# Seven half-size products in place of eight for the feed-forward gate units of a two-model forward pass

## The reference, cut to what matters

```python
D_MODEL = 1024; SEQ = 512; DEPTH = 2
D_FF = ((8 * D_MODEL // 3 + 255) // 256) * 256        # 2816

def swiglu(h, w_gate, w_up, w_down):
    return (jax.nn.silu(h @ w_gate) * (h @ w_up)) @ w_down

def first_block(x, ...):
    for i in range(DEPTH):
        h = rms_norm(x, mix_norm[i])
        x = x + (short_conv_mixer(...) if i % 2 == 0 else dilated_attention_mixer(...))
        h = rms_norm(x, ffn_norm[i])
        x = x + swiglu(h, ffn_w_gate[i], ffn_w_up[i], ffn_w_down[i])
    return rms_norm(x, final_norm)
```

## Time and profile before

| | |
|---|---|
| median of three runs | 2059.03 us (2058.18 to 2061.39) |
| the profiled execution | 2057.88 us |
| its span in the trace | 2055.9 us, so 2.0 us lie around the span |
| TensorE matmuls busy | 2024.0 us, 98% of the span |
| GpSimd busy | 1032.9 us, 50% |
| VectorE, ScalarE busy | 896.8 us, 840.8 us |
| gate and up of layer 0 / its down product | about 204 to 433 us / 433 to 553 us |
| the same of layer 1 | about 810 to 1040 us / 1040 to 1159 us |

### The profile page before, as it was taken

One profiled execution on the slowest core, in us unless ns is written; L12 is line 12 of the kernel. 1 busy time (PEld: TensorE's weight loads), 2 busy tenths in 40 slices (PEclk: granted clock), 3 DMA queues, 4 the chain that ended last, 5 costly groups with the idle time before them and its releaser, 6 DMA issues.

```text
span 2055.9 us, 25781 instructions
## 1 busy us (share of the span) xinstructions
PE 2024.0 (98%) x9884; PEld 1654.1 (80%) x9884; DVE 896.8 (44%) x1411; ACT 840.8 (41%) x1341; POOL 1032.9 (50%) x855
## 2 busy tenths in 40 slices
PE   9999999999999999999999999999999999999998
PEld 7888888888877777888888778988887876677787
DVE  3184433322144435334322388778875215443331
ACT  4123222222244443222222377677774325544543
POOL 4455544545532224544545468788885441323242
PEclk9999999999999999999999999999999999999999
DMA  5223233223433312333233334434432321112131
GB/s 169 97 87 113 83 103 103 84 84 97 126 91 93 92 42 82 103 103 102 84 89 101 102 105 123 122 104 114 133 103 62 105 84 62 60 63 81 43 103 62
DMA packets 259365, 193.28 MB, mean 94 GB/s; under 512 B 9459, under 2 KB 247335, under 8 KB 259256
## 3 DMA queue, kind: packets, MB, share of 16 engines
q1 hardware_dynamic: 256188, 190.67, 30.9%
q10 hardware_dynamic: 3068, 1.09, 0.2%
HBM read 189.46 MB, written 2.27 MB: 93 GB/s over the span
## 4 chain that ended last, share of the span: by engine, by line
PE 38%; issue 35%; POOL 21%; DVE 2%; ACT 2%; DMA 1%; POOLq 0%; SPq 0%; ACTq 0%; DVEq 0%
POOL wlo L652 21%; PE bank L2058 11%; PE bank L2060 11%; PE bank L2059 11%; PE bank L2541 1%; PE bank L2537 1%; PE bank L2505 1%; DMA raw<-in_conv_w_in 0%; DVE xc L1668 0%; ACT whi L741 0%; DVE hLo L1971 0%; DMA rows<-cums 0%; PE bank L2519 0%; PE bank L2493 0%; PE bank L2477 0%
## 5 line engine op out<-in xcount | busy, mean ns | idle before, releaser
L652 POOL TENSOR_TENSOR wlo<-raw,whi 128x512 fp32r<-128x512 f32 (+1 forms) x664 | 842.4, 1299 | 942.7 <-ACT whi L741 942.7
L2058 PE MATMUL bank<-hHi,whi 128*128 128x512 f32 (+1 forms) x1392 | 548.4, 394 | 3.8 <-DVE qk L1554 1.5
L2060 PE MATMUL bank<-hHi,wlo 128*128 128x512 f32 (+1 forms) x1392 | 540.7, 388 | 0.0
L2059 PE MATMUL bank<-hLo,whi 128*128 128x512 f32 (+1 forms) x1392 | 540.4, 388 | 0.0
L741 ACT ACTIVATE whi<-raw 128x2048 fp32r<-128x2048 f32 (+1 forms) x167 | 301.8, 1807 | 476.0 <-PE bank L2060 473.0
L2058 PEld LDWEIGHTS bank<-hHi,whi 128*128 128x128 f32 x1392 | 261.4, 188 | 63.2 <-issue 6.6
L2060 PEld LDWEIGHTS bank<-hHi,wlo 128*128 128x128 f32 x1392 | 261.3, 188 | 54.8
L2059 PEld LDWEIGHTS bank<-hLo,whi 128*128 128x128 f32 x1392 | 261.5, 188 | 53.2 <-issue 1.2
L2058 PE MATMUL bank<-whi,hHi 128*128 128x256 f32 (+1 forms) x640 | 219.4, 343 | 2.2 <-POOL wlo L652 1.8
L2060 PE MATMUL bank<-whi,hLo 128*128 128x256 f32 (+1 forms) x640 | 208.5, 326 | 0.0
L2059 PE MATMUL bank<-wlo,hHi 128*128 128x256 f32 (+1 forms) x640 | 208.3, 326 | 0.0
(11 more groups left out here) (387 smaller groups left out, 2930.7 us busy)
## 6 DMA issues: line engine op xcount, KB each, us to landing
raw<-in_ssd_w_in SPq DMA_DIRECT2D x48, 512.0 KB, 4.8
raw<-in_ffn_w_gate SPq DMA_DIRECT2D x44, 512.0 KB, 4.7
raw<-in_ffn_w_up SPq DMA_DIRECT2D x44, 512.0 KB, 4.7
raw<-in_gla_w_in SPq DMA_DIRECT2D x40, 512.0 KB, 4.6
rows<-cums SPq DMA_DIRECT2D x64, 256.0 KB, 5.4
raw<-in_ffn_w_down SPq DMA_DIRECT2D x32, 384.0 KB, 3.6
raw<-in_attn_w_qkv SPq DMA_DIRECT2D x24, 512.0 KB, 4.5
raw<-in_conv_w_in SPq DMA_DIRECT2D x23, 512.0 KB, 4.4
```

What stands on the lines that cost most here:

```text
L652: ins = pool.tensor_tensor(wlo[s][:, part], raw[s][:, part], whi[s][:, part].bitcast(F32), ALU.subtract)
L2058: pe.matmul(dst, hi1, hi2, start=first, stop=False)
L2059: pe.matmul(dst, hi1, lo2, start=False, stop=False)
L2060: return pe.matmul(dst, lo1, hi2, start=False, stop=last)
```

## The change

Pairs 3 to 10 of each feed-forward stage form the gate by seven products of half size (the scheme of Strassen and Winograd). The depth of 1024 is halved (kh = 0, 1), the 512 tokens are halved, and the 256 columns of the unit are its two halves m = 0, 1. Instead of eight products of 512 by 128 by 256 there are seven, of sums of weight quarters and of sums of token quarters. The up units keep their form but are cut in four quarters of weights too (u0 to u3). So a pair is 11 "turns" (`TURNS`), each with 128x512 elements of weights that pass ACT (`turn_high`), POOL (`turn_low`) and PE (`quarter`: 4 steps of depth, three parts, 12 matmuls; moving 256 columns for the seven, 512 for u0 to u3). `whi0` and `whi1` become eight slots for high parts, `wlo0` and `wlo1` eight for low parts; a turn's slot is free when PE is done with the turn eight places before.

```diff
+FIRST_SEVEN = 3
+TURNS = ["11", "12", "S2", "S1", "S3", "22", "u0", "S4", "u1", "u2", "u3"]
+SEVENS = FT // 2 - FIRST_SEVEN
+LOW_ON_POOL = [1, 3, 5, 7, 9, 15, 17, 19, 21]
+LOW_ON_DVE = [t for t in range(FT) if t not in LOW_ON_POOL]
```

On TensorE, in `ffn`:

```diff
+                def sevens(i):
+
+                    v, again = seven(j, i), i > FIRST_SEVEN
+                    if again:
+                        pe.wait_ge(*late("kept", 3 * v))
+                    else:
+                        pe.wait_ge(S(f"gs_ready{j}"), 2 * i + 1)
+                        pe.wait_ge(S(f"a_done{j}"), 2 * i + 1)
+                    quarter(bank[0], i, "11", half(0, 0), True, 256)
+                    if again:
+                        pe.wait_ge(*late("c_made", 4 * v))
+                    quarter(bank[2], i, "12", half(1, 0), True, 256)
+                    pe.wait_ge(*late("kept", 3 * v + 1))
+                    quarter(bank[0], i, "S2", summed(i, 2, 0), False, 256)
+                    quarter(bank[1], i, "S1", summed(i, 0, 1), True, 256)
+                    pe.wait_ge(*late("kept", 3 * v + 2))
+                    quarter(bank[0], i, "S3", summed(i, 1, 2), False, 256)
+                    quarter(bank[3], i, "22", summed(i, 3, 3), True, 256)
+                    if again:
+                        pe.wait_ge(S(f"a_done{j}"), 2 * i)
+                    quarter(bank[4], i, "u0", whole(0), True, SEQ, False)
+                    pe.wait_ge(*late("c_made", 4 * v + 2))
+                    quarter(bank[1], i, "S4", half(1, 1), False, 256)
+                    quarter(bank[4], i, "u1", whole(1), False, SEQ)
+                    if again:
+                        pe.wait_ge(S(f"a_done{j}"), 2 * i + 1)
+                    quarter(bank[5], i, "u2", whole(0), True, SEQ, False)
+                    quarter(bank[5], i, "u3", whole(1), False, SEQ)
```

On GpSimd, in `ffn`:

```diff
+                lows(u_up, u_up + 4)
+                for n, m in enumerate((1, 2, 0, 3)):
+                    token_sum_low(j, n, m)
+                    if n == 1:
+                        unit_low(u_up + 4)
+                unit_low(u_up + 5)
+                for i in range(FIRST_SEVEN, FT // 2):
+                    for name in TURNS:
+                        turn_low(j, i, name)
+                for t in LOW_ON_POOL[:3]:
+                    odd_low(j, t)
+                pool.sem_inc(w_lo, 2 * SEVENS)
+                low(u_down + 1, 0, DOWN)
+                for t in LOW_ON_POOL[3:5]:
+                    odd_low(j, t)
+                low(u_down + 2, 1, DOWN)
+                for t in LOW_ON_POOL[5:]:
+                    odd_low(j, t)
```

On ScalarE, in `ffn`:

```diff
+                def sevens(i):
+
+                    kept(i, 0, "11")
+                    turn_high(i, "u1")
+                    turn_high(i, "u2")
+                    kept(i, 1, "S2")
+                    turn_high(i, "u3")
+                    kept(i, 2, "S3")
+                    if i == FT // 2 - 1:
+                        for t in range(8):
+                            act_high(t)
+                        gate_silu(i, 0, 1)
+                        turn_down(0)
+                        gate_silu(i, 1, 0)
+                        for t in range(8, 19):
+                            act_high(t)
+                        turn_down(1)
+                        for t in range(19, FT):
+                            act_high(t)
+                        return
+                    turn_high(i + 1, "11")
+                    turn_high(i + 1, "12")
+                    gate_silu(i, 0, 1)
+                    gate_silu(i, 1, 0)
+                    for name in ("S2", "S1", "S3", "22", "u0", "S4"):
+                        turn_high(i + 1, name)
```

On VectorE, in `ffn`:

```diff
+                def sevens(i):
+
+                    more = i < FT // 2 - 1
+                    block(i, 0, 0, 0, bank[2], "12")
+                    block(i, 1, 1, 2, bank[1], "S1")
+                    block(i, 1, 0, 2, bank[3], "22")
+                    if more:
+                        first_sums(i + 1)
+                    scaled(i, 1, 3)
+                    if not more:
+                        even_lows(0, 2)
+                    block(i, 0, 1, 1, bank[1], "S4")
+                    scaled(i, 0, 4)
+                    if more:
+                        last_sums(i + 1)
+                    else:
+                        even_lows(2, 5)
+                    for b in range(2):
+                        dve.wait_ge(*late("q_mm", turned_by(j, i, f"u{2 * b + 1}")))
+                        up(i, b, bank[4 + b], 1 - b)
+                        if not more and b == 0:
+                            even_lows(5, 8)
```

More of the change, by code:

```diff
@@ L477, in _, with load @@
         def _(sp):
-            def load(n, s, src):
-                if not isinstance(n, int) or n >= 2:
+            def load(n, s, src, free=None):
+                if free is not None:
+                    for sem, count in free:
+                        sp.wait_ge(sem, count)
+                elif not isinstance(n, int) or n >= 2:
                     sp.wait_ge(w_lo, n - 1)
@@ new lines, in kept @@
+                def kept(i, n, name):
+                    act.wait_ge(*late("q_mm", turned_by(j, i, name)))
+                    copy(kept_part(j, i, n), bank[0][:, 0:256], L("kept"))
+                def sevens(i):
[23 more added lines that the diff above has]
+                        turn_high(i + 1, name)
@@ L884, in ffn @@
                 start_scale(2 * j + 1, u_up)
                 pair(0)
-                for i in range(1, FT // 2):
-                    pair(i)
+                for k in range(KT):
+                    copy(plain(j, 6 + k), tile(xT, k), L("xg_made"), scale=gain(2 * j + 1, k))
+                pair(1, token_highs)
+                pair(2)
+                for name in TURNS[:8]:
+                    turn_high(FIRST_SEVEN, name)
+                for i in range(FIRST_SEVEN, FT // 2):
+                    sevens(i)
@@ L1529, in ffn @@
+                pair(0)
+                token_sums()
+                for i in range(1, FIRST_SEVEN):
+                    pair(i)
+                for i in range(FIRST_SEVEN, FT // 2):
+                    sevens(i)
+                even_lows(8, len(LOW_ON_DVE))
                 for k in range(KT):
@@ L2261, in both, with quarter @@
                             mark(chan(bank[2 * s + b][:, :], s, pair(b), hHi, hLo, range(KT)))
-                for i in range(FT // 2):
+                def quarter(dst, i, name, moving, first, width, last=True):
+                    pe.wait_ge(*late("q_lo", turned_by(j, i, name)))
+                    hi, lo = slot(whi, j, i, name), slot(wlo, j, i, name)
+                    for n in range(4):
+                        w = slice(P * n, P * (n + 1))
+                        Hi, Lo = moving(n)
+                        to, begin = dst[:, 0:width], first and n == 0
+                        pe.matmul(to, hi[:, w], Hi, start=begin, stop=False, skip_group_check=True)
+                        pe.matmul(to, hi[:, w], Lo, start=False, stop=False, skip_group_check=True)
+                        ins = pe.matmul(to, lo[:, w], Hi, start=False, stop=last and n == 3, skip_group_check=True)
+                    ins.then_inc(L("q_mm"), 1)
```

211 lines of the change are left out of this document (188 added, 23 removed).

## The result

The kernel after takes 2061.6 us in the median (2058.55 to 2066.64), the kernel before, measured beside it, 2058.47 (2057.28 to 2061.43). The ratio is **1.0017 [1.0011, 1.0023]**: slower by some 3.5 us (3.1 by the medians), where I had forecast 2.8 us less. With 20 executions of either kernel this stands clear of the noise, though it is less than the 0.2% that I had taken for what a measurement can tell. The profiled execution after took 2060.44 us, with a span of 2058.7 against 2055.9, so the traces show about the same difference: +2.8.

A forecast was written before the change was run, and what follows sets the result against it. TensorE, busy 98% of the span at full clock, was taken as the bound; -12.8 (stream) + 3.6 (pair 3) + 0 + 6.4 (down product) = -2.8 us, from 2059.03 to 2056.2 us, range 2050.5 to 2062.

The forecast's parts named there:

- The stream: TensorE's matmuls in the 16 changed pairs: each pair 0.80 us shorter, -12.8 us in all.
- (E): Rival, changed pairs: half-wide matmuls cost more, at 0.1295 us no gain, 2069; chance 0.13 shared with (C) and anything slower.
- the one of open weight loads: Rival, changed pairs: 36 more weight loads a pair don't overlap matmuls, +109 us; chance under 1 in 100.
- Inside pairs 4 to 10: Middle of the feed-forward stage: helpers all stay below TensorE's 20.96 us a pair, so nothing comes late, 0.
- (C): Rival, `kept` handoff: ScalarE late at bank 0, 2072 at 0.5 us lateness; chance 0.13 shared with (E) and anything slower.
- Pair 3: Gate of pair 3 waits for both up tiles of pair 2: 1.8 us a layer, +3.6.
- the fork: Pair 3: whether DVE's scaling or GpSimd's subtraction goes first; DVE assumed, 3.0 us a layer as upper end.
- Pairs 0 to 2: Token sums before pair 2's gate just fit on the helpers: 0, up to 1.5 us a layer otherwise.
- The start of the down product: GpSimd's low parts make down unit 2 late: TensorE stands 3.2 us a layer, +6.4.
- (D): Rival, pair 3 and down product: both stops at upper ends, +5.0 at most, more likely +2, 2061; chance 0.10.
- (A): Rival, down product: GpSimd's backlog mostly hidden, stop about 1 us a layer, 2051.8; chance 0.30.
- (B): Rival, whole feed-forward stage: nothing comes late at all, `a_done` included, 2046.2; chance 0.05.

The follow-up runs named there:

- e5: Changed kernel, but GpSimd starts the low part of pair 3's turn S3 only after VectorE stored both up tiles of pair 2: 2058.4 us, ratio 1.0001.
- e2: Changed kernel, but VectorE instead of GpSimd makes the low parts of tiles 15, 17, 19 and 21: 2056.51 us, ratio 0.9984.
- e1: Changed kernel, but pair 3's gate waits for pair 2's up tiles one by one, ahead of turns 12 and 22: 2055.25 us, ratio 0.9977.
- e4: Kernel before, plus six idle GpSimd subtractions between the second and third down units of layer 0: 2062.89 us, ratio 1.0013.
- e6: Changed kernel with pair 3's wait split by tile and low parts of tiles 17, 19, 21 moved from GpSimd to VectorE: 2049.03 us, ratio 0.9952.

## Why the prediction was wrong

Point by point, in its order.

- **The stream, -12.8.** Right. Every pair of the eight shows 0.120 and 0.227 us a matmul, and 8 x 0.80 = 6.4 a layer is there; the two stretches differ by 6.0, as the restart behind the stop (0.1) and the changes of width lie in the later one. Rivals (E) and the one of open weight loads are out.
- **Inside pairs 4 to 10, 0.** Right but for 0.25 us a layer at the changes of width. The `kept` copy was to take under 0.5; it takes 0.38, starts close behind its bank's last matmul and no wait of TensorE for it is in the list, so (C) is out. GpSimd's subtractions took 1344 ns in the mean, where I had about 1.4 us. Timeline of ScalarE, kernel after:

```profile
283.14 0.38 ACT L909 ACTIVATE f0kept<-bank 128x256 f32<-128x256 f32 x1 [0.80 <-PE bank L2588]
286.02 0.38 ACT L909 ACTIVATE f0kept<-bank 128x256 f32<-128x256 f32 x1 [0.81 <-PE bank L2588]
```

- **Pair 3, +3.6.** The mechanism was right, with the right engine and queue, and the size wrong: +5.9. I had named the fork, DVE first or GpSimd first, given it 0.05 us, and taken the cheap side. ScalarE's copy for S3 started with VectorE's read, at 257.81 both, not 0.05 later, and GpSimd came 0.02 ahead. e5 measures the branch that I took (1.6 us of waiting), the kernel after the other (2.7). This is the first step that was mis-sized, by 2.3 us in all. With a margin of one reading error I should have booked the middle, 2.4 a layer.
- **Pairs 0 to 2, 0.** Right: no wait of TensorE there.
- **The start of the down product, +6.4.** The waiting is right: 2 x 2.7 by GpSimd at the third unit, and ready at D + 17.9 where I had 18.2. The pieces are priced right too: unit 1 took 5.21 and the four tiles 6.84, which is 3.4 us over the price alone, where I had 7 x 0.46 = 3.2. With the restart and the crumbs ahead it is 3.0 instead of 3.2. Seven operations of VectorE with two inputs in SBUF do fall beside these pieces, 0.49 each: this bears out the price by the row, 0.46 a collision, against the whole instruction; by 0.69 the stop would have been 1.6 longer.
- **The step that failed: the clock.** The working has no term for what a stop does to the granted clock. It said that TensorE is at the full clock everywhere, counted each stop at its own length, and so a stop of 2.7 us at the down product was 2.7 us; it costs 4.4. That is +3.4 in the sum: it alone takes the forecast from -2.8 to +0.6, and pair 3 does the rest. The full table of tenths in the earlier trace rows did not show it, before or after, as a slice of 51 us hides 1.7; the row of stretches of a few us does. Even the trace of before has one such place, which I had not looked for:

```profile
1538.40:1541.80 3.40, 3.06 (x7) 2.48 (x8) 3.40 (x4) 3.40 (x11) 3.01 (x3) 0.50 1.00 270
```

- **The sum.** -12.8 + 5.9 + 0.5 + 9.3 = +2.9, where I had -2.8: 2.3 of the 5.7 by pair 3, 2.9 by the down product (3.4 of clock, less 0.5), 0.5 by the pitches. The measured time is that of rival (D), 2061, but not by its way: only one of its two stops came out at its upper end, and the clock gave the rest. I gave it 0.10, since I treated two long stops as one unlucky case instead of asking what else a stop brings. (A) and (B), 0.35 together, rested on backlog or waits being hidden; the stop of 2.5 us at the third down unit speaks against both.

What stays open: why some stops of 2.7 us are followed by the half clock (e2 at pair 3, twice) and others of the same length at the same place are not (after, twice). The output projection has had a stop of 1.8 us for GpSimd all along (the longest in the earlier trace rows); the half clock follows it in e1, e4 and e6, and not in the other five traces. All stretches in the feed-forward stages begin during a stop of 2.0 to 2.7 us or within 1.4 us behind it, but I did not try what decides in each case.

## What to carry to other kernels

Give each new stop of TensorE in a dense stream two prices, its length and, for a stop of about 2 us or more, the 1.7 us that a stretch at the lower clock behind it may cost (here 9 of 11 stops of 2.0 to 2.7 us in the feed-forward stages had one, and 3 of 8 of 1.8 us at the output projection); where TensorE soon waits for a helper anyway, that price can be nothing, as at 1221.5. Look for such stretches in windows of a few us, since busy time and coarse slices don't show them. A change that speeds the stream by moving waits to the stage's edges should be given the waits at the point of first use (one wait in front of the bank that needs it, not in front of the first matmul): here that was worth at least as much as the choice of who does the helpers' work (0.9977 in e1 against 0.9984 in e2, with intervals that overlap), and the two together were worth most. Where two helpers start within a tenth of a microsecond of each other, book the mean of both orders.

## What I had not expected of the hardware

Behind stops of 1.8 to 2.7 us TensorE ran for 3.4 us, and once for 6.8, at a granted clock of 0.50: in the kernel after at 446.7 and 1054.3, in e4 at 450.4, in e2 at 260.3 and 867.9. And one VectorE operation of 128x512 that began 0.02 us behind a subtraction of GpSimd took 1.80 us instead of 0.69, which GpSimd's mean prices (1344 ns here, 1400 in the earlier trace rows) don't hint at.
